# A mixture-of-experts stage that works in blocks of 64 rows instead of 128

## The chip, the cores and the metric

The kernel runs on one NeuronCore of a Trainium2 chip, in one launch. The metric is the device time of that launch in microseconds (us); lower is better. All matrices are float32.

## The reference, cut to what matters

The whole program is three layers on 512 tokens of width 1024: two sequence-mixing layers with feed-forward blocks, and a third layer that ends in a mixture of experts. Only the mixture of experts is touched:

```python
def hier_moe(h, w_rg, b_rg, w_re, b_re, w_up, w_down):    # h (512, 1024)
    g_logits = (h @ w_rg + b_rg)                          # 4 groups of 8 experts
    g_sel = jnp.argmax(g_logits, axis=-1)                 # one group per token
    e_in = ...                                            # the 8 logits of that group
    top_v, top_i = lax.top_k(e_in, 2)                     # two experts per token
    w2 = jax.nn.softmax(top_v, axis=-1) * p_sel
    combine = ...                                         # (512, 32), two non-zero shares in a row
    out = jnp.zeros_like(h)
    for n in range(32):                                   # w_up (32, 1024, 512), w_down (32, 256, 1024)
        a, b = jnp.split(h @ w_up[n], 2, axis=-1)
        out = out + combine[:, n:n + 1] * ((jax.nn.silu(a) * b) @ w_down[n])
    return out
```

A token counts for two experts only, so there are 1024 pairs of a token and an expert. The weights of one expert are 2 MiB (up) and 1 MiB (down).

How the 1024 pairs spread over the experts follows from the inputs. The reference evaluated on its own inputs gives these counts for the 32 experts: 34 39 25 25 36 34 21 36 13 24 25 30 21 16 12 33 18 16 63 38 24 15 26 24 20 87 79 45 55 41 34 15. Every expert is used; the largest counts are 87, 79 and 63.

## The kernel before, in words

The last stage, `moe` (L3286), is four steps with a barrier between them.

`route` computes the logits and the two experts of every token, and stores the normalised token rows to a DRAM buffer, `normalised_rows`.

`place` (L2909) gives each pair a slot. The slots of an expert are cut into blocks of P = 128 rows; an expert with `count` tokens gets `count/128` blocks, rounded up. From comparisons (`blocks`, L2945 to L2948, one comparison for each block that an expert may need; `full`, L2970 to L2973, the same for the rank of a token) and running sums VectorE works out `r.row` (where the result of a pair will lie), `r.expert` (the expert of each block) and the one-hot matrices `is_slot` and `is_block`. TensorE multiplies the last two (L2931) into `r.token`, the token of each slot of each block. `NB` = 40 is the number of blocks provided for; `r.before_last` says how many pairs of blocks are really filled.

`experts` (L3013) works through the filled blocks. For a block n:

- SP loads the weights of the block's expert: `load_up` (L3066, 2 MiB) and `load_down` (L3069, 1 MiB), into two sides that alternate. The load of a side is issued when the matmuls that read it two blocks earlier are done. Each block loads its weights, also where two blocks have the same expert.
- POOL gathers the block's token rows by an indirect DMA from `normalised_rows` (L3117).
- PE transposes the rows (`turn_rows`, L3131), DVE copies them out of PSUM into `e.x` (`columns`, L3217). `first` (L3141) multiplies with the up weights: the rows are the stationary operand, the 512 columns of the weights move. ACT (silu, L3185) and DVE (`gated`, L3225) make the hidden rows; PE transposes these (`turn_hidden`, L3150), ACT copies them (L3194), and `second` (L3161) multiplies with the down weights, again with 512 moving columns at a time. ACT copies the result out (L3199), and SP stores it to the DRAM buffer `expert_results` (`store`, L3076).

PE's order is a software pipeline, written out by hand:

```python
            def step(n):
                if inside(n, 1):
                    first(later(n, 1))
                turn_hidden(n)
                if inside(n, 2):
                    turn_rows(later(n, 2))
                second(n)
```

`each_block` (L3037) runs the first pair of blocks, a hardware loop over the following pairs with a branch that skips those not filled, and the last filled pair. Before that, SP runs its own loop over all pairs (L3097 to L3103): for a pair that is not filled it writes zeros to `expert_results`, for a filled one it only counts a semaphore up.

`combine` (L3239) gathers the two result rows of every token by eight indirect DMAs and adds them with their shares to the residual.

Of the kernel before, what the change touches and what calls it, by code (L numbers as in the profile page):

```python
# [18 lines left out]
F32 = mybir.dt.float32  # L19
# [7 lines left out]
P = 128  # L27
# [2876 lines left out]
SLOTS = 2 * T  # L2904
NB = 2 * -(-((SLOTS + NE * (P - 1)) // P) // 2)
FTE = EF // P


def place(k, r, zeros):  # L2909

# [3 lines left out]
    with nc.Block(no_gpsimd_drain=True) as block:  # L2914
        @block.tensor
        def _(pe):
            ps = k.ps[:, 0, :]
            for t in range(NT):

                for before in range(t):  # L2920
                    nc.tensor.matmul(ps[:, t * NE:(t + 1) * NE], k.ones[:, :], r.both[:, before, :], start=(before == 0), stop=False, skip_group_check=True)
                nc.tensor.matmul(ps[:, t * NE:(t + 1) * NE], k.tri[0][:, :], r.both[:, t, :], start=(t == 0), stop=True, skip_group_check=True)
            for t in range(NT):
                nc.tensor.matmul(ps[:, NT * NE:(NT + 1) * NE], k.ones[:, :], r.both[:, t, :], start=(t == 0), stop=(t == NT - 1), skip_group_check=True)

            nc.tensor.matmul(ps[:, (NT + 1) * NE:(NT + 1) * NE + 1], k.tri[0][:, :], k.ones[:, 0:1], start=True, stop=True,
                             skip_group_check=True).then_inc(k.pa.sem, 1)

            pe.wait_ge(*k.va(1))
            for n in range(2 * NT):  # L2930
                last = nc.tensor.matmul(k.ps[:, 1, 0:NB], r.is_slot[:, n, :], r.is_block[:, n, :], start=(n == 0), stop=(n == 2 * NT - 1))  # L2931
            last.then_inc(k.pb.sem, 1)

        @block.vector
        def _(dve):
            nc.vector.memset(zeros[:, :], 0.0)
            ps = k.ps[:, 0, :]
            upto = ps[:, 0:NT * NE].rearrange("p (t e) -> p t e", t=NT)
# [6 lines left out]
            nc.vector.tensor_scalar(r.blocks[:, :], count, 0.0, None, ALU.is_gt)  # L2945
            for n in range(1, T // P):
                dve.drain()
                nc.vector.scalar_tensor_tensor(out=r.blocks[:, :], in0=count, scalar=float(n * P), in1=r.blocks[:, :], op0=ALU.is_gt, op1=ALU.add)  # L2948
            dve.drain()
# [17 lines left out]
            dve.drain()  # L2967
            nc.vector.scalar_tensor_tensor(out=r.row_f[:, :], in0=r.block[:, :], scalar=float(P), in1=r.rank[:, :], op0=ALU.mult, op1=ALU.add)

            nc.vector.tensor_scalar(r.full[:, :], r.rank[:, :], float(P), None, ALU.is_ge)  # L2970
            for n in range(2, T // P):
                dve.drain()
                nc.vector.scalar_tensor_tensor(out=r.full[:, :], in0=r.rank[:, :], scalar=float(n * P), in1=r.full[:, :], op0=ALU.is_ge, op1=ALU.add)  # L2973
            dve.drain()
            nc.vector.tensor_tensor(r.block[:, :], r.block[:, :], r.full[:, :], ALU.add)
            nc.vector.scalar_tensor_tensor(out=r.rank[:, :], in0=r.full[:, :], scalar=-float(P), in1=r.rank[:, :], op0=ALU.mult, op1=ALU.add)
            nc.vector.tensor_copy(r.row[:, :], r.row_f[:, :])
# [21 lines left out]
            dve.wait_ge(*k.pb(1))  # L2999
            nc.vector.tensor_copy(r.token[:, :], k.ps[:, 1, 0:NB])  # L3000
    k.pa.close(1)
# [11 lines left out]
def experts(k, r, rows_dram, y_dram, up, dn, e):  # L3013
# [43 lines left out]
    with nc.Block(no_gpsimd_drain=True) as block:  # L3057
        @block.sync
        def _(sp):
# [14 lines left out]
            def store(n):  # L3074
                sp.wait_ge(e.y_ready, at_block(n, 1, 1))
                sp.dma_start(y_dram[bass.ds(at_block(n, P), P), :] if isinstance(n, tuple) else y_dram[n * P:(n + 1) * P, :],  # L3076
                             e.y[:, side(n), :]).then_inc(e.y_ended if of_last_pair(n) else e.y_stored[side(n)], 16)

# [30 lines left out]
        @block.gpsimd  # L3109
        def _(pool):  # L3110
            def step(n):
                s = side(n)
                if not early(n, 2):
                    pool.wait_ge(e.turned, at_block(n, 1, -1))
                nc.gpsimd.tensor_copy(e.slot_token[:, s:s + 1], r.token[:, bass.ds(at_block(n), 1)] if isinstance(n, tuple) else r.token[:, n:n + 1])
                pool.drain()
                nc.gpsimd.indirect_dma_start(e.rows[:, s, :], None, rows_dram, bass.IndirectOffsetOnAxis(ap=e.slot_token[:, s:s + 1], axis=0))\  # L3117
                    .then_inc(e.gathered[s], 16)

            each_block(pool, pair_before_last(nc.gpsimd), step)  # L3120
            pool.drain()

        @block.tensor
        def _(pe):
# [9 lines left out]
            def first(n):  # L3134
                s = side(n)
                pe.wait_ge(e.x_ready, at_block(n, 1, 1))
                pe.wait_ge(e.up_loaded[s], pair(n, 16))
                if not early(n, 2):
                    pe.wait_ge(e.hidden, at_block(n, 1, -1))
                for c in range(KD):  # L3140
                    last = nc.tensor.matmul(k.ps[:, UB + s, :], e.x[:, s, c, :], up[s][:, c, :], start=(c == 0), stop=(c == KD - 1))  # L3141
                last.then_inc(e.up_done, 1)
# [10 lines left out]
            def second(n):  # L3153
# [5 lines left out]
                for half in range(2):  # L3159
                    for j in range(FTE):  # L3160
                        last = nc.tensor.matmul(k.ps[:, YB + half, :], e.hid_cm[:, s, j, :], dn[s][:, j, half * BANK:(half + 1) * BANK],  # L3161
                                                start=(j == 0), stop=(j == FTE - 1))
# [16 lines left out]
        def _(act):  # L3179
            def silu(n):  # L3180
                s = side(n)
                act.wait_ge(e.up_done, at_block(n, 1, 1))
                if not early(n, 2):
                    act.wait_ge(e.hidden, at_block(n, 1, -1))
                nc.scalar.activation(e.silu[:, s, :], k.ps[:, UB + s, 0:EF], ACT.Silu).then_inc(e.silu_ready, 1)  # L3185

            def step(n):
# [4 lines left out]
                if not early(n, 2):  # L3192
                    act.wait_ge(e.down_done, at_block(n, 1, -1))
                nc.scalar.copy(e.hid_cm[:, s, :, :], k.ps[:, HB, 0:EF].rearrange("p (j m) -> p j m", j=FTE)).then_inc(e.hid_ready, 1)  # L3194
                act.wait_ge(e.down_done, at_block(n, 1, 1))
                if not early(n, 2):
                    act.wait_ge(e.y_stored[s], at_block_pairs(n))
                for half in range(2):
                    last = nc.scalar.copy(e.y[:, s, half * BANK:(half + 1) * BANK], k.ps[:, YB + half, :])  # L3199
                last.then_inc(e.y_ready, 1)  # L3200
# [8 lines left out]
        def _(dve):  # L3209
            def columns(n):  # L3210
# [75 lines left out]
def moe(k, out):  # L3286

    nc, A, sb = k.nc, k.A, k.alloc
    with ExitStack() as c:
# [14 lines left out]
        r.token_id = sb("moe_token_id", [P, NT], to=c)  # L3304
        r.is_slot = sb("moe_is_slot", [P, 2 * NT, P], to=c)
        r.is_block = sb("moe_is_block", [P, 2 * NT, NB], to=c)
# [9 lines left out]
        e.rows = sb("expert_rows", [P, 2, D], to=c)  # L3316
        e.x = sb("expert_x", [P, 2, KD, P], to=c)
        e.silu = sb("expert_silu", [P, 2, EF], to=c)
        e.hid = sb("expert_hid", [P, 2, EF], to=c)
        e.hid_cm = sb("expert_hid_cm", [P, 2, FTE, P], to=c)  # L3320
        e.zeros = sb("zeros", [P, D], to=c)
# [14 lines left out]
        place(k, r, e.zeros)  # L3336
        experts(k, r, rows_dram, y_dram, up, dn, e)
# [46 lines left out]
```

## Time and profile before

| | us |
|---|---|
| median of 3 runs | 3220.49 |
| lowest, highest run | 3217.85, 3221.48 |
| span of the profiled execution (first to last instruction) | 3219.3 |
| its own time | not given beside the span; the span is 1.2 below the median of the runs |
| PE busy | 2712.0 (84%) |
| PE weight load busy | 2062.7 (64%) |
| DVE, ACT, POOL busy | 1439.6, 991.8, 1018.6 |
| mean granted TensorE clock | 0.875 of full speed |

The table gives the sums over the span. The expert stage is about the last 420 us of it, from the first weight load of the stage at 2799.3 us. Busy shares over the whole span say little of this stage, so views of the stage by itself are needed: the profile's 40 slices (each 80.5 us), busy times by stretch, and timelines. A matmul of float32 shows as two records.

### The profile page before, as it was taken

The page shows a single profiled execution, that of the slowest core. Times are in us where ns is not written, and L with a number is a line of the kernel's source. Part 1 is how long each engine was busy: PE and PEld are TensorE (multiplying, and loading weights), DVE is VectorE, ACT ScalarE, POOL GpSimd, SP SyncE. Part 2 cuts the span into 40 slices and gives each one's busy share as a digit, 9 for nine tenths or more (in the row PEclk, how much of TensorE's full clock was granted, in tenths as well). Part 3 has the DMA queues.
Part 4 walks back from the last instruction along what each step waited for, and adds up shares of the span by engine and source line. Part 5 has one row for each costly group of instructions (what it writes and reads, how often), then busy time and mean ns, then how long its engine had stood idle before and what let it go on. Part 6 is the DMA issues. An engine that isn't in the chain of part 4 may idle for free. (4 is left out here: it accounts for less than half of the span.)

```text
span 3219.3 us, 32244 instructions
## 1 busy us (share of the span) xinstructions
PE 2712.0 (84%) x11467; PEld 2062.7 (64%) x11467; DVE 1439.6 (45%) x2067; ACT 991.8 (31%) x1675; POOL 1018.6 (32%) x673
## 2 busy tenths in 40 slices
PE   6969696869799898947779989789795978599996
PEld 5859585657688786824568878577584667444442
DVE  4468405625544443034454444417896265411111
ACT  2233331033454324331244442433332342111111
POOL 2424342034444344412234434444250053001111
PEclk9979797779899998967789999799796589599998
DMA  2300020021233312210023332222030011299997
GB/s 90 105 27 1 31 74 1 1 105 66 72 98 91 117 66 79 79 54 1 13 63 94 98 106 84 92 80 96 26 105 26 1 69 39 101 362 369 369 365 260
DMA packets 203760, 319.88 MB, mean 99 GB/s; under 512 B 13269, under 2 KB 105309, under 8 KB 203517
## 3 DMA queue, kind: packets, MB, share of 16 engines
q1 hardware_dynamic: 197885, 297.39, 27.0%
q0 software_dynamic: 5760, 20.97, 1.7%
q8 instruction: 71, 1.16, 0.1%
q14 instruction: 44, 0.36, 0.0%
HBM read 293.17 MB, written 25.17 MB: 99 GB/s over the span
## 5 line engine op out<-in xcount | busy, mean ns | idle before, releaser
L357 POOL TENSOR_TENSOR w_lo<-ring,w_hi 128x512 fp32r<-128x512 f32 (+1 forms) x264 | 355.5, 1348 | 579.2 <-ACT w_hi L514 578.6
L514 ACT CAST w_hi<-ring 128x512 fp32r<-128x512 f32 (+1 forms) x264 | 163.1, 618 | 487.6 <-PE ps L364 446.0
L357 POOL TENSOR_TENSOR ffn_w_lo<-ring,ffn_w_hi 128x1024 fp32r<-128x1024 f32 x88 | 211.5, 2426 | 275.2 <-ACT ffn_w_hi L1689 275.2
L362 PE MATMUL ps<-w_hi,h_hi 128*128 128x512 f32 (+1 forms) x672 | 264.4, 393 | 33.3 <-DVE h_lo L357 33.0
L362 PE MATMUL ps<-ffn_h_hi,ffn_w_hi 128*128 128x512 f32 x704 | 278.0, 395 | 16.3 <-DVE ffn_h_lo L357 16.3
L363 PE MATMUL ps<-ffn_h_lo,ffn_w_hi 128*128 128x512 f32 x704 | 276.8, 393 | 0.0
L364 PE MATMUL ps<-ffn_h_hi,ffn_w_lo 128*128 128x512 f32 x704 | 276.6, 393 | 0.0
L362 PE MATMUL ps<-wo_hi,lhs_hi 128*128 128x512 f32 x608 | 241.3, 397 | 41.1 <-DVE lhs_lo L357 41.1
L357 POOL TENSOR_TENSOR wo_lo<-ring,wo_hi 128x1024 fp32r<-128x1024 f32 x76 | 186.4, 2458 | 275.7 <-ACT wo_hi L642 275.7
L363 PE MATMUL ps<-w_lo,h_hi 128*128 128x512 f32 (+1 forms) x672 | 262.6, 391 | 0.0
L364 PE MATMUL ps<-w_hi,h_lo 128*128 128x512 f32 (+1 forms) x672 | 262.3, 390 | 0.0
L363 PE MATMUL ps<-wo_lo,lhs_hi 128*128 128x512 f32 x608 | 240.4, 395 | 0.0
L364 PE MATMUL ps<-wo_hi,lhs_lo 128*128 128x512 f32 x608 | 239.8, 394 | 0.0
L3141 PE MATMUL ps<-ring,expert_x 128*128 128x512 f32 x512 | 229.9, 603 | 8.9 <-issue 6.1
L3141 PEld LDWEIGHTS ps<-ring,expert_x 128*128 128x128 f32 x512 | 98.8, 194 | 134.2 <-issue 130.8
L362 PEld LDWEIGHTS ps<-w_hi,h_hi 128*128 128x128 f32 x672 | 128.4, 191 | 64.5 <-POOL w_lo L357 38.7
L362 PEld LDWEIGHTS ps<-ffn_h_hi,ffn_w_hi 128*128 128x128 f32 x704 | 133.7, 190 | 48.8 <-issue 11.1
L357 DVE TENSOR_TENSOR lhs_lo<-ffn_g,lhs_hi 128x512 fp32r<-128x512 f32 x44 | 110.1, 2509 | 119.5 <-ACT lhs_hi L643 119.5
L1731 DVE SCALAR_TENSOR_TENSOR y_tmp<-ps,pcol,y_tmp 128x511 f32<-128x511 f32 x88 | 61.9, 746 | 220.1 <-ACT y_tmp L1694 220.1
L362 PEld LDWEIGHTS ps<-wo_hi,lhs_hi 128*128 128x128 f32 x608 | 116.6, 192 | 67.5 <-POOL wo_lo L357 42.8
L642 ACT CAST wo_hi<-ring 128x1024 fp32r<-128x1024 f32 x76 | 79.7, 1049 | 258.1 <-PE ps L364 253.5
L362 PE MATMUL ps<-h_hi,w_hi 128*128 128x512 f32 x352 | 142.3, 404 | 16.7 <-DVE h_lo L357 16.0
(529 smaller groups left out, 5282.0 us busy)
## 6 DMA issues: line engine op xcount, KB each, us to landing
ring<-in_w_up SPq DMA_DIRECT2D x32, 2048.0 KB, 12.1
ring<-in_ffn_w_up SPq DMA_DIRECT2D x88, 512.0 KB, 4.9
moe_down<-in_w_down SPq DMA_DIRECT2D x32, 1024.0 KB, 10.1
ring<-in_ab_w_in SPq DMA_DIRECT2D x13, 2048.0 KB, 7.8
ring<-in_w_in SPq DMA_DIRECT2D x11, 2048.0 KB, 7.8
ring<-in_ffn_w_down SPq DMA_DIRECT2D x10, 2048.0 KB, 8.0
expert_results<-expert_y SPq DMA_DIRECT2D x32, 512.0 KB, 10.2
ring<-in_c_w_in SPq DMA_DIRECT2D x6, 2048.0 KB, 8.3
```

The lines of the kernel that those rows point to most:

```text
L357: return engine.tensor_tensor(lo, whole, hi.bitcast(F32), ALU.subtract)
L362: nc.tensor.matmul(out, left[0], right[0], start=start, stop=False, **more)
L363: nc.tensor.matmul(out, left[0], right[1], start=False, stop=False, **more)
L364: return nc.tensor.matmul(out, left[1], right[0], start=False, stop=stop, **more)
L514: nc.scalar.copy(part(w_hi, p), chunk(j)[:, rows, cols]).then_inc(k.w_hi_ready.sem, 1)
L642: nc.scalar.copy(w_hi[:, n % PIECES, :], weights(n)).then_inc(k.w_hi_ready.sem, 1)
L1731: nc.vector.scalar_tensor_tensor(out=ybuf[:, s, half, 1:T], in0=bank(s, half)[:, 0:T - 1], scalar=column(tap0, i, s, half), in1=ybuf[:, s, ...
L3141: last = nc.tensor.matmul(k.ps[:, UB + s, :], e.x[:, s, c, :], up[s][:, c, :], start=(c == 0), stop=(c == KD - 1))
```

## The change: blocks of 64 rows

A constant `ROWS` = 64 takes the place of P = 128 wherever a block's height is meant. `NB`, the number of blocks provided for, becomes 48. Each expert with more than 64 tokens now takes two blocks, and each of these loads the expert's weights. The weights, the moving columns of the matmuls and the order of the work on each engine stay. The gather, the store, the silu, the product and the copies of the result work on 64 partitions; the copies of `e.x` and `e.hid_cm` take half of the columns. The two kinds of transposes still turn full 128-row tiles, whose lower half is set to zero once, by two memsets in `place`. `place` has four more comparisons for `blocks` and four more for `full`. `combine` is as before.

```diff
 SLOTS = 2 * T
-NB = 2 * -(-((SLOTS + NE * (P - 1)) // P) // 2)
+ROWS = 64
+NB = 2 * -(-((SLOTS + NE * (ROWS - 1)) // ROWS) // 2)
...
-                last = nc.tensor.matmul(k.ps[:, 1, 0:NB], r.is_slot[:, n, :], r.is_block[:, n, :], ...)
+                last = nc.tensor.matmul(k.ps[0:ROWS, 1, 0:NB], r.is_slot[:, n, :], r.is_block[:, n, :], ...)
...
             nc.vector.memset(zeros[:, :], 0.0)
+            nc.vector.memset(rows[ROWS:P, :, :], 0.0)
+            nc.vector.memset(hid[ROWS:P, :, :], 0.0)
...
-            for n in range(1, T // P):
+            for n in range(1, T // ROWS):
                 dve.drain()
-                nc.vector.scalar_tensor_tensor(out=r.blocks[:, :], in0=count, scalar=float(n * P), ...)
+                nc.vector.scalar_tensor_tensor(out=r.blocks[:, :], in0=count, scalar=float(n * ROWS), ...)
...
-            for n in range(2, T // P):
+            for n in range(2, T // ROWS):
                 dve.drain()
-                nc.vector.scalar_tensor_tensor(out=r.full[:, :], in0=r.rank[:, :], scalar=float(n * P), ...)
+                nc.vector.scalar_tensor_tensor(out=r.full[:, :], in0=r.rank[:, :], scalar=float(n * ROWS), ...)
...
-                nc.vector.tensor_scalar(r.is_slot[:, n, :], r.iota[:, :], r.rank[:, n:n + 1], None, ALU.is_equal)
+                nc.vector.tensor_scalar(r.is_slot[:, n, :], r.iota[:, 0:ROWS], r.rank[:, n:n + 1], None, ALU.is_equal)
...
-                             e.y[:, side(n), :]).then_inc(...)
+                             e.y[0:ROWS, side(n), :]).then_inc(...)
...
-                    sp.dma_start(y_dram[bass.ds(i * (2 * P) + 2 * P, 2 * P), :].rearrange("(s p) d -> p s d", p=P),
-                                 e.zeros[:, :].rearrange("p (o d) -> p o d", o=1).to_broadcast([P, 2, D])).then_inc(e.y_zeroed, 16)
+                    sp.dma_start(y_dram[bass.ds(i * (2 * ROWS) + 2 * ROWS, 2 * ROWS), :].rearrange("(s p) d -> p s d", p=ROWS),
+                                 e.zeros[0:ROWS, :].rearrange("p (o d) -> p o d", o=1).to_broadcast([ROWS, 2, D])).then_inc(e.y_zeroed, 16)
...
-                nc.gpsimd.indirect_dma_start(e.rows[:, s, :], None, rows_dram, ...e.slot_token[:, s:s + 1]...)
+                nc.gpsimd.indirect_dma_start(e.rows[0:ROWS, s, :], None, rows_dram, ...e.slot_token[0:ROWS, s:s + 1]...)
...
-                    last = nc.tensor.matmul(k.ps[:, UB + s, :], e.x[:, s, c, :], up[s][:, c, :], ...)
+                    last = nc.tensor.matmul(k.ps[0:ROWS, UB + s, :], e.x[:, s, c, :], up[s][:, c, :], ...)
...
-                        last = nc.tensor.matmul(k.ps[:, YB + half, :], e.hid_cm[:, s, j, :], dn[s][:, j, half * BANK:(half + 1) * BANK], ...)
+                        last = nc.tensor.matmul(k.ps[0:ROWS, YB + half, :], e.hid_cm[:, s, j, :], dn[s][:, j, half * BANK:(half + 1) * BANK], ...)
...
-                nc.scalar.activation(e.silu[:, s, :], k.ps[:, UB + s, 0:EF], ACT.Silu).then_inc(e.silu_ready, 1)
+                nc.scalar.activation(e.silu[0:ROWS, s, :], k.ps[0:ROWS, UB + s, 0:EF], ACT.Silu).then_inc(e.silu_ready, 1)
...
-                nc.scalar.copy(e.hid_cm[:, s, :, :], k.ps[:, HB, 0:EF].rearrange("p (j m) -> p j m", j=FTE)).then_inc(e.hid_ready, 1)
+                nc.scalar.copy(e.hid_cm[:, s, :, :], k.ps[:, HB, 0:EF].rearrange("p (j m) -> p j m", j=FTE)[:, :, 0:ROWS]).then_inc(e.hid_ready, 1)
...
-                    last = nc.vector.tensor_copy(e.x[:, s, c, :], k.ps[:, XB + half, :].rearrange("p (c m) -> p c m", c=NT))
+                    last = nc.vector.tensor_copy(e.x[:, s, c, :], k.ps[:, XB + half, :].rearrange("p (c m) -> p c m", c=NT)[:, :, 0:ROWS])
...
-                nc.vector.tensor_tensor(e.hid[:, s, :], e.silu[:, s, :], k.ps[:, UB + s, EF:2 * EF], ALU.mult).then_inc(e.hidden, 1)
+                nc.vector.tensor_tensor(e.hid[0:ROWS, s, :], e.silu[0:ROWS, s, :], k.ps[0:ROWS, UB + s, EF:2 * EF], ALU.mult).then_inc(e.hidden, 1)
...
-        y_dram = nc.dram_tensor("expert_results", (NB * P, D), F32, kind="Internal").ap()
+        y_dram = nc.dram_tensor("expert_results", (NB * ROWS, D), F32, kind="Internal").ap()
```

## Rows read from the trace of the kernel before

**Rows 1.** The page: granted TensorE clock and DMA rate in 40 slices.

```profile
PEclk9979797779899998967789999799796589599998
GB/s 90 105 27 1 31 74 1 1 105 66 72 98 91 117 66 79 79 54 1 13 63 94 98 106 84 92 80 96 26 105 26 1 69 39 101 362 369 369 365 260
```

**Rows 2.** Stretches: PE, PEld, DVE, ACT, POOL busy us (count), clock, DMA share, GB/s.

```profile
3000.00:3050.00 50.00, 50.00 (x148) 24.45 (x147) 7.99 (x14) 7.99 (x18) 5.67 (x10) 1.00 1.01 373
...
2825.00:2830.00 5.00, 5.00 (x14) 2.19 (x13) 0.00 (x0) 0.00 (x0) 0.00 (x0) 1.00 1.03 415
```

**Rows 3.** Timeline of one block on PE: start us, us, engine, line, operation.

```profile
3003.01 7.03 PE L3141 MATMUL ps<-ring,expert_x 128*128 128x512 f32 x16
...
3009.87 0.38 PE L3150 MATMUL ps<-ident,expert_hid 128*128 128x128 f32 x2
...
3010.09 1.04 PE L3131 MATMUL ps<-ident,expert_rows 128*128 128x128 f32 x8
...
3010.97 3.60 PE L3161 MATMUL ps<-moe_down,expert_hid_cm 128*128 128x512 f32 x8
3014.40 7.03 PE L3141 MATMUL ps<-ring,expert_x 128*128 128x512 f32 x16
```

**Rows 4.** Timeline: an early and the last issue of an up load, 26 blocks apart.

```profile
2862.09 0.37 SPq L3066 DMA_DIRECT2D ring<-in_w_up  x1
...
3158.34 0.37 SPq L3066 DMA_DIRECT2D ring<-in_w_up  x1
```

**Rows 5.** DMA issues of the stage: count, KB each, median us to landing.

```profile
ring<-in_w_up SPq DMA_DIRECT2D x32, 2048.0 KB, 12.1
...
expert_results<-expert_y SPq DMA_DIRECT2D x32, 512.0 KB, 10.2
...
expert_rows<-normalised_rows,expert_slot_token POOLq DMA_INDIRECT x32, 8.0
```

**Rows 6.** Matmuls on 128 and on 16 stationary columns: duration ns min/median/max.

```profile
L3141 PE MATMUL ps<-ring,expert_x x512: 592/592/1219, 2811.6 to 3180.4; 128*128 128x512 f32 x171
...
L478 PE MATMUL ps<-h_cm,ring x32: 592/593/603, 1379.4 to 1392.7; 128*16 128x512 f32 x32
```

**Rows 7.** Timeline of the start of the experts, up to the third block's matmuls.

```profile
2811.57 9.05 PE L3141 MATMUL ps<-ring,expert_x 128*128 128x512 f32 x16 [1.38 <-DVE expert_x L3217]
...
2818.85 4.06 SPq L3099 DMA_DIRECT2D expert_results<-zeros  x4
...
2824.70 6.51 SPq L3066 DMA_DIRECT2D ring<-in_w_up  x2
...
2830.94 3.60 PE L3161 MATMUL ps<-moe_down,expert_hid_cm 128*128 128x512 f32 x8
...
2840.68 9.84 PE L3141 MATMUL ps<-ring,expert_x 128*128 128x512 f32 x16 [6.15 <-issue]
```

**Rows 8.** The zero fill's issues on SP: durations in ns, first and last start.

```profile
L3099 SPq DMA_DIRECT2D expert_results<-zeros x4: 383/404/432, 2818.9 to 2822.5; - x4
```

**Rows 9.** Timeline of the step that places the slots.

```profile
2777.88 0.91 DVE L2936 MEMSET zeros<- 128x1024 f32 x1 [0.97 <-PEq L2805]
...
2783.85 0.19 DVE L2945 TENSOR_SCALAR moe_blocks<-ps 128x32 f32<-128x32 f32 x1 [4.48 <-PE ps L2926]
2784.13 0.72 DVE L2948 SCALAR_TENSOR_TENSOR moe_blocks<-ps,moe_blocks 128x32 f32<-128x32 f32 x3
...
2788.00 0.41 DVE L2973 SCALAR_TENSOR_TENSOR moe_full<-moe_rank,moe_full 128x8 f32<-128x8 f32 x2
...
2792.57 1.49 DVE L2986 TENSOR_TENSOR moe_ended<-moe_block_end,moe_iota 128x1280 f32<-128x1280 f32 x1
2794.11 3.49 PEld L2931 LDWEIGHTS ps<-moe_is_block,moe_is_slot 128*128 128x128 f32 x16 [10.38 <-DVE moe_ended L2986]
...
2797.79 0.20 DVE L3000 CAST moe_token<-ps 128x40 int32<-128x40 f32 x1 [1.27 <-PE ps L2931]
```

**Rows 10.** Landing times of the result stores: min/median/max us.

```profile
DMA to landing us min/median/max: 2.7/10.2/15.3
```

More of the change, by code:

```diff
@@ L2904, with place @@
 SLOTS = 2 * T
-NB = 2 * -(-((SLOTS + NE * (P - 1)) // P) // 2)
+ROWS = 64
+NB = 2 * -(-((SLOTS + NE * (ROWS - 1)) // ROWS) // 2)
 FTE = EF // P
-def place(k, r, zeros):
+def place(k, r, zeros, rows, hid):
     nc = k.nc
@@ L2930, in _ @@
             for n in range(2 * NT):
-                last = nc.tensor.matmul(k.ps[:, 1, 0:NB], r.is_slot[:, n, :], r.is_block[:, n, :], start=(n == 0), stop=(n == 2 * NT - 1))
+                last = nc.tensor.matmul(k.ps[0:ROWS, 1, 0:NB], r.is_slot[:, n, :], r.is_block[:, n, :], start=(n == 0), stop=(n == 2 * NT - 1))
             last.then_inc(k.pb.sem, 1)
@@ L2945, in _ @@
             nc.vector.tensor_scalar(r.blocks[:, :], count, 0.0, None, ALU.is_gt)
-            for n in range(1, T // P):
+            for n in range(1, T // ROWS):
                 dve.drain()
-                nc.vector.scalar_tensor_tensor(out=r.blocks[:, :], in0=count, scalar=float(n * P), in1=r.blocks[:, :], op0=ALU.is_gt, op1=ALU.add)
+                nc.vector.scalar_tensor_tensor(out=r.blocks[:, :], in0=count, scalar=float(n * ROWS), in1=r.blocks[:, :], op0=ALU.is_gt, op1=ALU.add)
             dve.drain()
@@ L2999, in _ @@
             dve.wait_ge(*k.pb(1))
-            nc.vector.tensor_copy(r.token[:, :], k.ps[:, 1, 0:NB])
+            nc.vector.tensor_copy(r.token[0:ROWS, :], k.ps[0:ROWS, 1, 0:NB])
     k.pa.close(1)
@@ L3114, in step @@
                     pool.wait_ge(e.turned, at_block(n, 1, -1))
-                nc.gpsimd.tensor_copy(e.slot_token[:, s:s + 1], r.token[:, bass.ds(at_block(n), 1)] if isinstance(n, tuple) else r.token[:, n:n + 1])
+                nc.gpsimd.tensor_copy(e.slot_token[0:ROWS, s:s + 1], r.token[0:ROWS, bass.ds(at_block(n), 1)] if isinstance(n, tuple) else r.token[0:ROWS, n:n + 1])
                 pool.drain()
-                nc.gpsimd.indirect_dma_start(e.rows[:, s, :], None, rows_dram, bass.IndirectOffsetOnAxis(ap=e.slot_token[:, s:s + 1], axis=0))\
+                nc.gpsimd.indirect_dma_start(e.rows[0:ROWS, s, :], None, rows_dram, bass.IndirectOffsetOnAxis(ap=e.slot_token[0:ROWS, s:s + 1], axis=0))\
                     .then_inc(e.gathered[s], 16)
@@ L3140, in first @@
                 for c in range(KD):
-                    last = nc.tensor.matmul(k.ps[:, UB + s, :], e.x[:, s, c, :], up[s][:, c, :], start=(c == 0), stop=(c == KD - 1))
+                    last = nc.tensor.matmul(k.ps[0:ROWS, UB + s, :], e.x[:, s, c, :], up[s][:, c, :], start=(c == 0), stop=(c == KD - 1))
                 last.then_inc(e.up_done, 1)
@@ L3160, in second @@
                     for j in range(FTE):
-                        last = nc.tensor.matmul(k.ps[:, YB + half, :], e.hid_cm[:, s, j, :], dn[s][:, j, half * BANK:(half + 1) * BANK],
+                        last = nc.tensor.matmul(k.ps[0:ROWS, YB + half, :], e.hid_cm[:, s, j, :], dn[s][:, j, half * BANK:(half + 1) * BANK],
                                                 start=(j == 0), stop=(j == FTE - 1))
@@ L3198, in step @@
                 for half in range(2):
-                    last = nc.scalar.copy(e.y[:, s, half * BANK:(half + 1) * BANK], k.ps[:, YB + half, :])
+                    last = nc.scalar.copy(e.y[0:ROWS, s, half * BANK:(half + 1) * BANK], k.ps[0:ROWS, YB + half, :])
                 last.then_inc(e.y_ready, 1)
@@ L3304, in moe @@
         r.token_id = sb("moe_token_id", [P, NT], to=c)
-        r.is_slot = sb("moe_is_slot", [P, 2 * NT, P], to=c)
+        r.is_slot = sb("moe_is_slot", [P, 2 * NT, ROWS], to=c)
         r.is_block = sb("moe_is_block", [P, 2 * NT, NB], to=c)
@@ L3333, in moe @@
         rows_dram = nc.dram_tensor("normalised_rows", (T, D), F32, kind="Internal").ap()
-        y_dram = nc.dram_tensor("expert_results", (NB * P, D), F32, kind="Internal").ap()
+        y_dram = nc.dram_tensor("expert_results", (NB * ROWS, D), F32, kind="Internal").ap()
         route(k, wr, r, k.ytmp[:, :, :], rows_dram)
-        place(k, r, e.zeros)
+        place(k, r, e.zeros, e.rows, e.hid)
         experts(k, r, rows_dram, y_dram, up, dn, e)
```

16 lines of the change are left out of this document (8 added, 8 removed).

## The prediction, made before the changed kernel ran

> **What bounds the kernel now.** I read the 40 slices first. In the last five the DMA rate jumps from about 100 to 360 to 370 GB/s [rows 1]: this is the expert stage, and at first sight it is bound by transfers. The second view corrects that. In the 50 us from 3000 the DMA engines are busy all the time (share 1.01), but PE is busy for 50.00 of 50.00 us too, at the full granted clock (1.00, the 2.4 GHz level) [rows 2]. Two resources at 100% need a third view that tells which one sets the pace. In the timeline of one block the matmuls of `first` start at 3003.01, the transposes of the hidden rows at 3009.87, those of the token rows at 3010.09, `second` at 3010.97, and the next `first` at 3014.40 [rows 3]. Nowhere does a row of PE carry a wait for a DMA. The steps add up by themselves: 16 records of `first` in 6.86 us are 0.429 us each; 8 of `second` in 3.43 us are 0.429 each; the ten transposes take 1.10 us. That is 11.39 us, the whole period. Over 26 blocks the period does not vary: (3158.34 - 2862.09) / 26 = 11.394 us [rows 4].
>
> The transfers have slack that the share of 1.01 hides. A block moves 2 MiB + 1 MiB of weights, 0.5 MiB of gathered rows and 0.5 MiB of results, 4.19 MB, in 11.39 us: 368 GB/s. Shortly after the start of the stage the same engines moved 415 GB/s [rows 2]. An up load is issued when `first` of its side is done and is needed 11.39 + 4.3 = 15.7 us later; it lands after 12.1 us [rows 5]. So PE bounds the steady part, and the transfers follow some 10% behind as second. Only at the start do transfers bind: PE has finished `second` of block 0 at about 2834.5, waits 6.15 us, and starts block 2's `first` at 2840.68 [rows 7].
>
> **The change part by part.**
>
> *Number of blocks.* The counts of tokens of the experts are 87 and 79 for two, 63 or less for the others. At 128 rows that is 32 blocks, as the 512 records of L3141 (16 for a block) show [rows 6]. At 64 rows it is 34 blocks, 17 pairs, so nothing is lost to pairing.
>
> *Time of a block on PE.* The rows are the stationary operand and the weights move, so the 64 rows halve the loaded columns, not the 512 that move. The trace has the same matmul with 16 stationary columns: 593 ns, against 592 ns with 128 [rows 6]. 32 of them start within 1379.4 to 1392.7, 13.3 us / 31 = 0.429 us apart, the cadence of the expert matmuls. The weight load of 0.19 us lies beneath them (PE weight load 24.45 of 50 us [rows 2]) and shortening it gives nothing. The transposes still turn 128 rows, so their 1.10 us stay. A block costs 11.39 us as before. Bounds: the row with 16 columns leaves no room above or below; I give it 0.05 us either way.
>
> *What gets shorter and lies aside.* The copies of `e.x` and of `e.hid_cm`, silu and the product run on ACT and DVE, which are each busy for 7.99 of 50 us [rows 2]: worth nothing. The gather and the store move half of the bytes. A block moves 3.67 MB in place of 4.19, 322 GB/s at the period of 11.39 us. PE does not wait for these transfers now, so their relief in the steady part is worth nothing as well. All in all the stage moves 34 x 3.67 MB = 124.8 in place of 134.2 MB, 7% less, and this shows only in the DMA columns.
>
> *Sum of the steady part:* 2 x 11.394 = +22.8 us.
>
> *Start of the stage.* Here bytes count, until block 2's up weights land. What SP does there: its loop counts filled pairs (now 16 at the head of the loop instead of 15) and then issues a zero fill for each pair that is not filled. Provided are 24 pairs, 17 filled, so 7 fills of 0.5 MiB instead of 4 of 1 MiB: 3.67 against 4.19 MB. The fills start 1.2 us apart (2818.9 to 2822.5 for four [rows 8]), so the last of seven starts three steps, 3.6 us, later, and the up load queued behind them is issued at about 2829 instead of 2824.70 [rows 7].
> Lower end: 64-row transfers run at the full rate of about 0.4 MB/us. Up to block 2's first matmul 0.52 MB of fills and four gathers of 0.26 MB fall away, 1.57 MB or 3.9 us. By 2829 the queue has just run dry, the load takes 2.1 / 0.4 = 5.2 us and some 2 us to land: 2836.3, 4.4 us earlier than now. After so short a wait the granted clock might stay at full; now block 2's `first`, behind its wait of 6.15 us, takes 9.84 us against 7.03 for a steady one [rows 3, 7], another 2.8 us. Together -7.2 us.
> Upper end: each 64-row transfer takes as long as its counterpart of 128 rows. Then the seven fills take 7/4 of the four: four are 4.19 MB / 0.4 = 10.5 us, seven are 18.3 us. From 2819.5 they end at about 2838, gathers in between 2838.5, the load lands about 2845: +4.3 us.
> The two ends are 11.5 us apart, and the trace has no transfer of such size on 64 partitions. The nearest row is the wait as it is, 6.15 us: fewer bytes on one side, more and later issues on the other. I take 0 and keep -7.2 and +4.3.
>
> *Placing the slots.* These are in series with the whole stage. Four more comparisons for `blocks`: three of them take 2784.13 to 2784.93 with their drains, 0.27 each, so +1.07. Four more for `full` at 0.245 each (L2973 has two in 0.49 us): +0.98. `ended` grows from 1280 to 1536 elements: 1.49 x 48/40 = +0.30 [rows 9]. Against that the eight comparisons into `is_slot` are half as wide (0 to -0.5, I take -0.3), and the product at L2931 loads 64 columns: its 3.49 us of weight loads may fall to half, but then DVE's reduction and four small operations beside it (together 1.8 + 0.9 us after the signal) end last. Of the 3.7 us from signal to copy [rows 9] up to 0.9 can go; I take -0.6. The two memsets (2048 and 512 elements in the lower partitions, by the 0.91 us for 1024 about 1.8 + 0.5 us) fall into the 4.48 us for which DVE waits for PE [rows 9]: nothing, and their cover is twice what they need. Sum +1.4 us, between +0.6 and +2.4.
>
> *End of the stage.* Before `combine` can gather, the last store has to land; unhindered that takes 2.7 us for 0.5 MiB [rows 10]. With half the bytes 0 to -0.7 us: I take -0.2. `combine` reads the same 4 MiB as before.
>
> *Sum:* 22.8 + 0 + 1.4 - 0.2 = +24.0 us. Against the profiled span of 3219.3 this gives 3243.3; the span is 1.2 below the runs' median of 3220.49, which is within their spread of 3.6, so I add it: **3244.5 us**, 0.75% slower.
>
> **The rivals.**
>
> *A. The start gains.* The 64-row transfers run at the full rate, and the wait before block 2 all but disappears: 22.8 - 7.2 + 1.4 - 0.4 = +16.6, 3237 us. For it: the bytes. Against it: the seven issues of SP.
>
> *B. A 64-row transfer takes as long as one of 128 rows.* Then the seven fills hold the queue for 18.3 us: 22.8 + 4.3 + 1.4 = +28.5, 3249 us. In the steady part nothing changes: gather and store then take what they take now, and PE does not wait for that. The trace speaks neither for nor against. The Trainium skill does: its page "SBUF — State Buffer", section "Door 1: The DMA port swizzle", says that partitions 0 to 63 reach only 8 of the 16 ports, so that such a transfer runs at about half of the rate. By that rule the result is this rival's; no run here shows it yet.
>
> *C. The other sign: transfers set the period, not PE.* If the matmuls with 64 stationary columns ran faster, or if PE's records only looked full while it waited for weights, the period would follow the bytes: 3.67/4.19 x 11.39 = 9.98 us, and 34 x 9.98 = 339 against 32 x 11.39 = 364.5 us: -25 + 1.4, about 3197 us. It decides from the point where the cadence falls below 0.370 us for a record. For it: the DMA share of 1.01. Against it: no wait for a DMA in a steady block, a period constant to 0.01 us, and the row with 16 columns at the same duration.
>
> *D. It does not do what it says.* The expert with 63 tokens is one short of the edge. If rounding moved two tokens to it, there would be 35 blocks, 18 pairs, 36 blocks run: +22.8 more, 3267 us. The margins between second and third choice in that group are wide (one token under 0.09), so this is unlikely.
>
> **How the numbers follow.** Forecast 0.42 (own range 3240 to 3247), A 0.20, B 0.26, C 0.05, D 0.03, others 0.04, in which half is slower. The range goes from below A to above B with the bounds of the placing step: 3233 to 3253. Within 0.2% (6.4 us, about what a measurement tells from no change) is nearly none of them: 0.02. Faster 0.06, the rest slower, 0.92.
>
> **What would show it.** In the changed kernel: 544 records of L3141, 34 up loads and 7 zero fills; a period of 11.39 us between issues of L3066, with PE at 50.00 of 50 us and a rate near 322 GB/s; records of `first` and `second` still 0.429 us apart; the third block's `first` at about its present distance from the stage's first load, 41.4 us (A: 37, B: 46); 1.4 us more from the first comparison of `blocks` to the copy of `r.token`. A DMA share clearly below 1 in the steady part speaks against B, one that stays at 1 for it. A wait for a DMA in a steady block, or a period other than 11.39, would make the prediction wrong.

## The result and the profile after

| | before | after |
|---|---|---|
| median of 4 runs, us | 3220.98 | 3262.38 |
| lowest, highest | 3217.85, 3222.75 | 3260.06, 3262.77 |
| ratio to before, 95% interval | | 1.0128 [1.0114, 1.0142] |
| span of the profiled execution | 3219.3 | 3258.3 |
| records of the up matmuls, zero fills | 512, 4 | 544, 7 |

The changed kernel is 41.4 us slower, 39.0 us by the two profiled spans. 18 us of that were not in the forecast of 3244.5, and the time lies above the stated range.

The first view is the middle of the stage in busy times by stretch, with the columns of [rows 2]; behind it, from the timeline, an early and the last issue of an up load, 28 blocks apart.

```profile
3000.00:3050.00 50.00, 50.00 (x145) 18.14 (x144) 4.67 (x12) 7.85 (x18) 4.42 (x8) 1.00 0.97 320
...
2868.18 0.39 SPq L3069 DMA_DIRECT2D ring<-in_w_up  x1
...
3195.41 0.38 SPq L3069 DMA_DIRECT2D ring<-in_w_up  x1
```

PE is busy for 50.00 of 50 us at full clock, and the rate has fallen from 373 to 320 GB/s: all as forecast. But the period is (3195.41 - 2868.18) / 28 = 11.687 us, not 11.394 [rows 4]. The count of records says it too: 145 fit into 50 us in place of 148. The timeline of one block on PE (the counterpart of [rows 3]) shows where the 0.29 us lie:

```profile
3001.20 7.03 PE L3144 MATMUL ps<-ring,expert_x 128*64 128x512 f32 x16
...
3008.16 0.44 PE L3153 MATMUL ps<-ident,expert_hid 128*128 128x128 f32 x2
...
3008.43 1.04 PE L3134 MATMUL ps<-ident,expert_rows 128*128 128x128 f32 x8
...
3009.40 3.65 PE L3164 MATMUL ps<-moe_down,expert_hid_cm 128*64 128x512 f32 x8
...
3012.89 7.03 PE L3144 MATMUL ps<-ring,expert_x 128*64 128x512 f32 x16
```

From start to start the four steps take 6.96, 0.27, 0.97 and 3.49 us; before they took 6.86, 0.22, 0.88 and 3.43. Within `first` nothing changed, its records are still 0.429 us apart. The difference sits where the shape of the weights changes between 128*64 and 128*128, and the row of weight loads (PEld) tells what happens there. First the kernel before, then the one after, around the start of the transposes of the hidden rows:

```profile
3009.45 0.14 PEld L3150 LDWEIGHTS ps<-ident,expert_hid 128*128 128x128 f32 x1 [0.24 <-issue]
3009.88 0.14 PEld L3150 LDWEIGHTS ps<-ident,expert_hid 128*128 128x128 f32 x1 [0.29 <-issue]
```

```profile
3007.21 0.14 PEld L3144 LDWEIGHTS ps<-ring,expert_x 128*64 128x64 f32 x1 [0.29 <-issue]
3008.16 0.20 PEld L3153 LDWEIGHTS ps<-ident,expert_hid 128*128 128x128 f32 x2 [0.81 <-issue]
```

Before, the first transpose starts at 3009.87 and its weights were loaded from 3009.45, beneath the last matmul of `first`. After, the last load of `first` is at 3007.21, and the next begins at 3008.16, together with the transpose that it belongs to. No load was drawn ahead across the change of width, and the array waits for it. The way back, from the transposes to `second`, costs as much: of the 0.29 us, 0.15 lie in the first two steps (0.10 and 0.05) and 0.15 in the last two (0.09 and 0.06). PE's own busy row hides this, because a matmul's record goes on to its modelled end: 50.00 of 50 us in both kernels.

The trace of the kernel before has such a seam too, in front of the run of 16 columns in [rows 6]:

```profile
1378.85 0.19 PEld L364 LDWEIGHTS ps<-w_hi,h_lo 128*128 128x128 f32 x1
1379.07 0.39 PE L364 MATMUL ps<-w_hi,h_lo 128*128 128x512 f32 x1
1379.39 0.11 PEld L478 LDWEIGHTS ps<-h_cm,ring 128*16 128x16 f32 x2 [0.35 <-issue]
```

The records of 128 columns start 0.227 us apart there, each load one record ahead. The first load of 16 columns starts together with its own matmul at 1379.39, 0.09 us behind the point (1379.30) that the cadence gives. It is a single case in which other things change as well, so it proves nothing by itself, but it was the place to look.

The start of the stage, from the timeline (the counterpart of [rows 7]), and the stretch in which the fills run:

```profile
2819.16 13.63 SPq L3102 DMA_DIRECT2D expert_results<-zeros  x7
...
2834.88 3.04 SPq L3069 DMA_DIRECT2D ring<-in_w_up  x2
...
2846.67 9.63 PE L3144 MATMUL ps<-ring,expert_x 128*64 128x512 f32 x16 [13.36 <-issue]
...
2825.00:2830.00 5.00, 5.00 (x20) 2.13 (x19) 0.64 (x2) 0.64 (x2) 0.10 (x1) 1.00 0.98 246
```

The same five microseconds that moved 415 GB/s before [rows 2] move 246 GB/s, with the engines as busy (0.98). The seven issues take 13.63 us in all, more than seven steps of 1.2 us would be [rows 8]; I read this as SP waiting for room in its queue, and zeros_32_96 bears on it below. Block 2 starts 47.7 us behind the first load of the stage (2798.96), where it was 41.4.

The placing step, from its timeline (the counterpart of [rows 9]), and the last row of this section, a pause that the kernel before does not have:

```profile
2782.86 1.79 DVE L2951 SCALAR_TENSOR_TENSOR moe_blocks<-ps,moe_blocks 128x32 f32<-128x32 f32 x7
...
2787.79 1.37 DVE L2976 SCALAR_TENSOR_TENSOR moe_full<-moe_rank,moe_full 128x8 f32<-128x8 f32 x6
...
2794.90 1.94 PE L2932 MATMUL ps<-moe_is_block,moe_is_slot 128*64 128x48 f32 x16 [12.35 <-DVE moe_ended L2989]
...
2797.49 0.19 DVE L3003 CAST moe_token<-ps 64x48 int32<-64x48 f32 x1
```

```profile
3213.38 7.08 PE L3144 MATMUL ps<-ring,expert_x 128*64 128x512 f32 x16 [1.66 <-issue]
```

From the first comparison to the copy of `r.token` it is 14.9 us against 13.9 [rows 9]. The pause of 1.66 us stands in front of the last block's `first`, where PE's loop has just passed over the pairs that are not filled.

The 39.0 us between the spans by landmark: up to the stage's first load -0.3 (this execution ran 1.3 us ahead before placing began, which itself took 1.0 longer); from there to block 2's `first` +6.3; from there to the last `second` +33.3, of which two blocks of 11.69 are 23.4, the longer periods of the others 8.2 (28 x 0.293), and the pause is 1.7; behind that -0.3. The runs' medians differ by 2.4 us more; the profiled execution was the shortest of its kernel (3260.06), the others took 3262.4 to 3262.8.

### The profile page after: what moved, and what is told of

It reads as the page before. It is cut to its first block and busy times, and to the rows that moved or that the text cites. A ratio compares the mean times of both kernels' runs of the same rounds, so it can differ in the third digit from the quotient of the medians.

```text
span 3258.3 us, 32594 instructions
## 1 busy us (share of the span) xinstructions
PE 2742.2 (84%) x11535; PEld 2025.9 (62%) x11535; DVE 1429.2 (44%) x2083; ACT 992.8 (30%) x1683; POOL 1013.6 (31%) x677
## 5 line engine op out<-in xcount | busy, mean ns | idle before, releaser
L3144 PE MATMUL ps<-ring,expert_x 128*64 128x512 f32 x544 | 243.5, 601 | 16.7 <-issue 15.0
L3144 PEld LDWEIGHTS ps<-ring,expert_x 128*64 128x64 f32 x544 | 75.2, 139 | 179.0 <-issue 176.7
L3228 DVE TENSOR_TENSOR expert_hid<-expert_silu,ps 64x256 f32<-64x256 f32 x34 | 14.0, 412 | 356.9 <-ACT expert_silu L3188 356.9
```

The costliest lines, as they stand in the source:

```text
L3144: last = nc.tensor.matmul(k.ps[0:ROWS, UB + s, :], e.x[:, s, c, :], up[s][:, c, :], start=(c == 0), stop=(c == KD - 1))
L3228: nc.vector.tensor_tensor(e.hid[0:ROWS, s, :], e.silu[0:ROWS, s, :], k.ps[0:ROWS, UB + s, EF:2 * EF], ALU.mult).then_inc(e.hidden, 1)
```

## Experiments

Two theories for the period: W, PE draws no weight load ahead over a change between 64 and 128 stationary columns; D, the 64-partition transfers or the shorter copies shift the block's timing. For the start: P, transfers on partitions 0 to 63 are slow; I, seven issues of SP set it. Times are medians, with the ratio to the kernel before on the same chip; that kernel took 3221.46 in the first four experiments and 3220.26 in the others. Where a time is set against the changed kernel (3262.38, beside 3220.98 for the kernel before), the two come from different series, and such a difference of 4 us alone is not clear of the spread; there the distances within the traces decide.

### full_width: both matmuls load 128 columns again

```diff
-        e.x = sb("expert_x", [P, 2, KD, ROWS], to=c)
+        e.x = sb("expert_x", [P, 2, KD, P], to=c)
-                    last = nc.tensor.matmul(k.ps[0:ROWS, UB + s, :], e.x[:, s, c, :], up[s][:, c, :], ...)
+                    last = nc.tensor.matmul(k.ps[:, UB + s, :], e.x[:, s, c, :], up[s][:, c, :], ...)
... (the same for e.hid_cm and second; both copies take all columns)
```

> The changed kernel, but the copies into e.x and e.hid_cm take all 128 columns again and the matmuls of first and second load 128 stationary columns (the upper 64 are the zero rows); gather, silu, product and store stay at 64 rows. Theory W (the period grew from 11.39 to 11.69 us because PE changes between 64 and 128 stationary columns twice in a block, and a weight load is not drawn ahead over such a change): the period is 11.39 us again, the first load of the transposes starts 0.4 us before they do, and the run is 34 x 0.29 = 10 us faster than the changed kernel, about 3252 us. Rival D (the transfers on 64 partitions, or the shorter copies, shift the block's timing): the period stays at 11.69 us and the time at 3262. The start of the stage is not touched: block 2's first matmul 47.7 us behind the first load in both.

Measured: 3254.06 us, ratio 1.0094 [1.0074, 1.0113], 8.3 us faster than the changed kernel. The issues of the up loads are back at (3190.79 - 2871.75) / 28 = 11.394 us, and in the timeline of the weight loads the one for the first transpose is drawn ahead again: it starts at 3007.70, the transpose at 3008.13:

```profile
3007.70 0.14 PEld L3153 LDWEIGHTS ps<-ident,expert_hid 128*128 128x128 f32 x1 [0.24 <-issue]
3008.13 0.14 PEld L3153 LDWEIGHTS ps<-ident,expert_hid 128*128 128x128 f32 x1 [0.29 <-issue]
```

The transfers were as in the changed kernel, so they are not the cause; the copies were whole again, and that half of D is left to the next experiment. Block 2 starts 48.0 us behind the first load, so the start is as it was. The 10 us expected were too many: the seams of blocks 0 and 1 lie ahead of block 2's wait, which hides them, and in the last two blocks PE waits for ACT anyway. From block 2's `first` to the last `second` of the changed kernel they cost 8.8 us (30 x 0.293), and the pause before the last block grew from 1.66 to 1.95 us, by just what the period lost. That leaves 8.5 us, and 8.3 were measured.

### narrow_before: only the width, in the kernel before

```diff
-                    last = nc.tensor.matmul(k.ps[:, UB + s, :], e.x[:, s, c, :], up[s][:, c, :], ...)
+                    last = nc.tensor.matmul(k.ps[0:64, UB + s, :], e.x[:, s, c, 0:64], up[s][:, c, :], ...)
... (the same for second)
```

> The kernel before (blocks of 128 rows, 32 blocks, all transfers on 128 partitions), but first and second load only 64 stationary columns and write 64 rows; the upper half of each block is left out of these matmuls. Theory W: the period becomes 11.69 us with nothing else changed, 32 x 0.29 = +9.5 us on the time before, about 3230. Rival D: 11.39 us and 3221.

Measured: 3230.92 us, ratio 1.0029 [1.0015, 1.0044], +9.5 us. The period is (3165.74 - 2861.88) / 26 = 11.687 us. So the width alone, with 128-row transfers, whole copies, 32 blocks and everything else as before, gives the changed kernel's period to the last digit, and D falls. That the time meets the 9.5 us so exactly is in part luck: from block 2's `first` to the last `second` the trace is 8.3 us longer, and the interval reaches from 5 to 14 us. The kernel leaves out the upper half of each block, so it serves as a measurement only.

### second_full: one of the two matmuls wide

```diff
-                        last = nc.tensor.matmul(k.ps[0:ROWS, YB + half, :], e.hid_cm[:, s, j, :], ...)
+                        last = nc.tensor.matmul(k.ps[:, YB + half, :], e.hid_cm[:, s, j, :], ...)
... (e.hid_cm with P columns, copied whole)
```

> The changed kernel with 128 stationary columns in second alone (e.hid_cm copied whole); first keeps 64. If each change of width costs (theory W), there are still two in a block, from first to the transposes and from second to first: the period stays at 11.65 to 11.7 us, the gap at the transposes stays, the one between the transposes and second goes and a new one stands between second and first. If it is the narrow matmuls that cost, 8 of 24 records are wide again and the period falls to about 11.6 us or, if the cost is in second alone, to 11.5. Time 3262 by W, 3256 to 3259 by the other.

Measured: 3265.72 us, ratio 1.0137 [1.0119, 1.0154], not told apart from the changed kernel's 1.0128 [1.0114, 1.0142]; period (3193.02 - 2865.73) / 28 = 11.689 us. A third of the narrow records is gone and nothing is won: the cost is by change of width, two in a block, about 0.147 us each, and not by narrow matmul. The weight loads show the gap moved from the front of `second` to its end:

```profile
3009.46 0.19 PEld L3164 LDWEIGHTS ps<-moe_down,expert_hid_cm 128*128 128x128 f32 x1 [0.24 <-issue]
3010.41 0.19 PEld L3144 LDWEIGHTS ps<-ring,expert_x 128*64 128x64 f32 x2 [0.76 <-issue]
```

### zeros_128: the fills read 128 partitions

```diff
-                    sp.dma_start(y_dram[...].rearrange("(s p) d -> p s d", p=ROWS),
-                                 e.zeros[0:ROWS, :].rearrange("p (o d) -> p o d", o=1).to_broadcast([ROWS, 2, D])).then_inc(e.y_zeroed, 16)
+                    sp.dma_start(y_dram[...], e.zeros[:, :]).then_inc(e.y_zeroed, 16)
```

> The changed kernel, but each zero fill of two blocks (128 result rows, 0.5 MiB) reads 128 partitions in place of twice 64; count, bytes and place of the fills stay. Theory P (a transfer on partitions 0 to 63 runs at about half of the rate: the trace shows 206 to 263 GB/s while the fills run, against 391 to 415 before the change): the rate returns to about 400 GB/s, the seven issues take some 8 us instead of 13.6, the up load behind them is issued at 29 to 30 us behind the first load of the stage instead of 35.9, and block 2 starts 37 to 39 us behind it instead of 47.7; with the clock kept at full 9 to 12 us faster than the changed kernel, about 3252. Rival I (seven issues of SP set it): block 2 starts at 46 to 48 us as now, and the time stays at 3262. The period stays at 11.69 us.

Measured: 3257.78 us, ratio 1.0112 [1.0095, 1.0130]. Two rows of the timeline and one stretch:

```profile
2819.20 7.29 SPq L3102 DMA_DIRECT2D expert_results<-zeros  x7
...
2828.50 2.11 SPq L3069 DMA_DIRECT2D ring<-in_w_up  x2
...
2825.00:2830.00 5.00, 5.00 (x13) 1.43 (x12) 0.00 (x0) 0.00 (x0) 0.00 (x0) 1.00 1.02 389
```

The seven issues take 7.29 us, the rate is 389 GB/s, and the up load goes out 30.1 us behind the first load (2798.39), all as P says; I falls as the whole cause. The edit changes two things, though: the partitions, and one run for each fill in place of two. The next experiment parts them. The next step of the expectation was wrong: block 2 starts at 2842.15, 43.8 us behind the first load, not 37 to 39. The up load needs 13.7 us from issue to use, where I had counted some 8, as for a transfer by itself. In a steady block of the changed kernel an up load lands after 11.0 us (median), with the other transfers beside it. Nor did the clock stay up: block 2's `first` takes 9.82 us. The start wins 3.9 us. That is clear of its own noise (47.7, 48.0 and 48.2 us in the traces of the changed kernel, full_width and second_full), and about what the medians show (4.6). 2.4 us of the start's loss stay (43.8 against 41.4 in the kernel before): the up load still goes out 30.1 us behind the first load, where it was 25.4.

### zeros_32_96: the same fills from other partitions

```diff
-                                 e.zeros[0:ROWS, :].rearrange("p (o d) -> p o d", o=1)...
+                                 e.zeros[32:32 + ROWS, :].rearrange("p (o d) -> p o d", o=1)...
```

> The changed kernel, with one edit: the 64 partitions that each zero fill reads are 32 to 95 in place of 0 to 63. Shape, bytes, count and place of the fills are unchanged. Theory P1 (it matters which partitions: 0 to 63 reach half of the ports, 32 to 95 all of them): the seven issues take 7.3 us as with 128 partitions instead of 13.6, the rate while they run is 370 to 390 GB/s, and block 2 starts about 43.8 us behind the first load instead of 47.7; 4 us faster than the changed kernel. Rival P2 (it matters that there are only 64 partitions, or two runs for each): issues 13.6 us, 206 to 263 GB/s, 47.7 us, the same time as the changed kernel.

Measured: 3258.83 us, ratio 1.0120 [1.0104, 1.0137], 3.5 us below the changed kernel. The last three lines are the fills' issues by themselves, in ns (minimum, median, maximum), of the changed kernel, zeros_128 and this one.

```profile
2821.11 9.40 SPq L3102 DMA_DIRECT2D expert_results<-zeros  x7
...
2844.26 9.82 PE L3144 MATMUL ps<-ring,expert_x 128*64 128x512 f32 x16 [9.34 <-issue]
...
2825.00:2830.00 5.00, 5.00 (x12) 1.37 (x10) 0.00 (x0) 0.00 (x0) 0.93 (x1) 1.00 1.01 364
...
L3102 SPq DMA_DIRECT2D expert_results<-zeros x7: 619/1339/1794, 2819.2 to 2831.0; - x7
...
L3102 SPq DMA_DIRECT2D expert_results<-zeros x7: 332/332/402, 2819.2 to 2826.2; - x7
...
L3102 SPq DMA_DIRECT2D expert_results<-zeros x7: 607/607/776, 2821.1 to 2829.9; - x7
```

Same shape, same bytes, same number of partitions, and 364 GB/s in place of 246. Block 2 starts 43.8 us behind the first load (2800.47), like zeros_128. The issues took 9.4 us, more than the 7.3 I had written and less than 13.6. Their single durations say why: a fill in two runs of 64 partitions takes SP 0.61 us to issue where one of 128 partitions takes 0.33, and that is the 2.1 us to zeros_128. In the changed kernel the shortest issue takes 0.62 us as well, the median one 1.34: the 4.2 us more come with the slow transfers, which fits SP waiting for room. So it matters which 64 partitions a transfer touches, and P2 falls but for the dearer issue. The section "Door 1: The DMA port swizzle" of "SBUF — State Buffer" in the Trainium skill has this: partitions 0 to 63 reach 8 of the ports, and by its table of ports 32 to 95 reach all 16. The traces agree in kind; the pure rate of such a fill was not isolated, since gathers ran beside it.

### nb36: room for 36 blocks

```diff
-NB = 2 * -(-((SLOTS + NE * (ROWS - 1)) // ROWS) // 2)
+NB = 36
```

> The changed kernel with room for 36 blocks instead of 48, enough for the 34 of these inputs: one pair is skipped and filled with zeros in place of seven. Theory S (the start's loss is the fills ahead of block 2's load; the pause of 1.66 us on PE before the last block's matmuls is the seven skipped turns of its loop): the up load is issued about 24.5 us behind the first load instead of 35.9, block 2 starts at 34 to 36 us instead of 47.7 with the clock at full (2.6 us more), the pause before the last block is gone (-1.7), placing is 0.5 us shorter: 16 to 19 us faster than the changed kernel, 3243 to 3246. Rival: the start is bound by the weights and gathers themselves and stays above 43 us, or the pause has another cause and stays; then 3255 or more. The period stays at 11.69 us.

Measured: 3242.65 us, ratio 1.0067 [1.0049, 1.0085], 20 us faster than the changed kernel by the medians and 17 by the profiled spans, at the edge of the 16 to 19 expected. The up load goes out 22.4 us behind the first load, earlier than expected. In the timeline block 2 starts 34.7 us behind the first load (2799.65) with no wait before it and at full clock, and the last block follows without a pause:

```profile
2834.31 7.03 PE L3144 MATMUL ps<-ring,expert_x 128*64 128x512 f32 x16
...
3196.59 7.03 PE L3144 MATMUL ps<-ring,expert_x 128*64 128x512 f32 x16
```

(3196.59 - 2834.31) / 31 = 11.686 us: from block 2 to block 33 nothing is left but the period. The size of the provision, `NB`, had cost about 16 us at the start (13.0 of waiting and 2.6 of clock) and 1.7 us at the end. 36 fits only these inputs, so this is an experiment and not a version to use.

### late_zeros_before: the fills behind the last weight load

The kernel before, with its loop of fills moved behind the last weight load, between the two last blocks' steps on SP. The counting loop stays where it was.

```diff
         step((before, 2, 4))
+        between()
         step((before, 3, 4))
...
-                with sp.If(before < i):
-                    sp.dma_start(y_dram[...]..., e.zeros...).then_inc(e.y_zeroed, 16)
...
+            def fill():
+                with sp.Fori(0, NB // 2 - 1) as i:
+                    with sp.If(before < i):
+                        sp.dma_start(y_dram[...]..., e.zeros...).then_inc(e.y_zeroed, 16)
-            each_block(sp, before, step)
+            each_block(sp, before, step, fill)
```

> The kernel before (128 rows) with the four zero fills issued after the last weight load of the stage, when the transfer engines run empty, instead of ahead of block 2's load. Theory S: block 2's wait of 6.15 us goes and its first matmuls run at full clock (-2.8 us), the last stores come 0 to 2 us later: 7 to 9 us faster than the kernel before, about 3212. Rival: block 2's load is late for another reason (the weights of blocks 0 and 1 and the gathers), and the wait stays above 4 us; then no more than 2 us are won, or the fills delay the last stores by what is won at the start.

Measured: 3215.79 us, ratio 0.9984 [0.9975, 0.9993], the fastest of all, by 2 to 8 us below the kernel before. Block 2's wait is gone: three `first` follow at 2823.56, 2835.05 and 2846.45 at full clock. But the fills are not free at the end:

```profile
2835.05 7.03 PE L3146 MATMUL ps<-ring,expert_x 128*128 128x512 f32 x16
...
3175.20 4.01 SPq L3105 DMA_DIRECT2D expert_results<-zeros  x4
...
3192.47 0.94 POOL L3253 DMA_INDIRECT ring<-expert_results,moe_row  x1 [50.89 <-PEq L3248]
```

`combine`'s first gather comes 13.9 us behind the start of the last `second` (3178.55); in the kernel before it was 9.5 us (3196.51 - 3186.98). The end waits for the last stores and for 4 MiB of zeros: in the 5 us from 3180 the transfer engines are full (share 1.02, 405 GB/s), where in the kernel before they moved 105 GB/s in the 5 us from 3185. 4.4 of the 9 us won at the start are given back. The expectation of 0 to 2 us was too low, and the net of 4.5 us falls short of the 7 to 9 expected.

### late_full: both repairs in the 64-row kernel

The edits of full_width, zeros_128 and the late fills together.

> The 64-row kernel with both repairs: 128 stationary columns in first and second, and the zero fills on 128 partitions behind the last weight load. What is left over the kernel before with late fills is the two blocks (22.8 us), the placing (1.0) and the pause of 1.9 us before the last block. Expected 3236 to 3240, some 25 us above the kernel before with late fills. If the transfers that are saved were worth anything once the start is free of fills, it would be closer than 20 us.

Measured: 3238.74 us, ratio 1.0053 [1.0038, 1.0068]. That is 23.0 us above late_zeros_before, where the two blocks alone are 22.8. The pause before the last block is still there:

```profile
3193.00 7.13 PE L3148 MATMUL ps<-ring,expert_x 128*128 128x512 f32 x16 [1.95 <-issue]
...
3206.12 3.70 PE L3168 MATMUL ps<-moe_down,expert_hid_cm 128*128 128x512 f32 x8 [1.28 <-ACT expert_hid_cm L3201]
...
3216.03 0.96 POOL L3255 DMA_INDIRECT ring<-expert_results,moe_row  x1 [49.10 <-PEq L3250]
```

That the total comes to just the two blocks is a balance of other terms. By the traces, from block 2's `first` to the last `second` it is 25.0 us longer than late_zeros_before (two blocks, and the pause); up to block 2's `first` it is 2.6 longer; and from the last `second` to `combine`'s first gather it takes 9.9 us instead of 13.9, 4.0 less. There, behind the last weight load, fewer bytes (3.67 MB of zeros in place of 4.19, stores of half the size) may be worth something; the fills are also issued 1.5 us earlier against the last `second`, and no run separates the two. In the steady part the bytes that are saved bring nothing: the period is 11.394 us with either.

## Why the prediction was wrong, point by point

*PE bounds the stage.* Right. With 12% fewer bytes in a block the stage did not get faster, and rival C fell.

*Number of blocks, +22.8.* Right: 34 blocks, 17 pairs, two more periods. Rival D, more blocks than 34, did not occur.

*Time of a block on PE, "11.39 us as before ... 0.05 us either way".* This step failed, and it is the largest miss: the period grew by 0.293 us, 8.8 us over the 30 blocks in which no wait hides it. The row with 16 stationary columns was read rightly: the cadence inside a run of equal matmuls does not depend on the width. But [rows 6] are a run of one shape. I took from it that "shortening the weight load gives nothing" and did not ask what lies at the seams, where a block now goes from 64 to 128 columns and back. narrow_before and full_width show that the seams are all of it, second_full that it is the change of width that costs. The start of that very run, at 1379.39, had the sign of it.

*Start of the stage, taken as 0 between -7.2 and +4.3.* This term failed as well. It measured +6.3, above the upper end. The larger part of it, 3.9 us, is rival B's mechanism, shown by zeros_128 and zeros_32_96: fills from partitions 0 to 63 run slowly and hold the queue. The other 2.4 us stay with fast fills; there the up load goes out 4.7 us later than in the kernel before, behind seven issues in place of four, and the saved bytes do not make up for it. I had both mechanisms and the bound of 18.3 us for the fills, and took the middle without a row for it. The 2.0 us beyond that bound are not separated further: SP's seven issues took 13.6 us, so the up load went out at 2834.88 and not at 2829, and block 2 started 11.8 us behind it, where I had given a load 7 us by itself.

*Placing, +1.4.* It measured +1.0, within its bounds; the product that makes `r.token` took 1.94 us in place of 3.64, and DVE ended last, as described. *End, -0.2.* -0.3. The two memsets were hidden: DVE still waited for 1.55 us afterwards.

*Not in the sum at all: the pause of 1.66 us.* PE's loop skips seven unfilled pairs instead of four. I had counted the skipped turns for SP alone. There is no pause with four skipped pairs (the kernel before) or one (nb36), and with seven it stays when the fills are moved away (late_full, 1.95 us). What PE's queue does in such a turn no run shows.

By the profiled spans, +39.0 against +24.0, the miss of 15.0 us is: seams 8.8, start 6.3, pause 1.7, placing -0.4, end -0.1, and -1.3 by which this execution was ahead before the stage. Rival B came closest with 3249; B with the seams (8.8) and the pause (1.7) is 3259.5, and with the 2.0 us more at the start 3261.5.

## What to carry to other kernels

Cutting a block's height pays only if the height is what is paid for. Where the rows are the stationary operand and the weights move, a half-filled block costs the same on TensorE (0.429 us a record at 128, 64 and 16 columns here), and each extra block costs a full period; count the blocks first. When one operand's shape shrinks, look at the seams between instructions of different shape: padding the narrow operand back to the common width can be the faster form. Ask also of a transfer that keeps its bytes but loses partitions, and of every bound that a provision such as `NB` puts on loops that run in front of the real work.

## What the runs showed of the hardware that was not expected

A change between 64 and 128 stationary columns costs about 0.147 us at full clock, in either direction, beside matmuls of 512 moving columns: periods of 11.686 to 11.689 us in six kernels with two changes in a block, 11.394 us in the kernel before, full_width, late_zeros_before and late_full with none. The load behind the change starts together with its own matmul (both at 3008.16 in the changed kernel, and both at 3009.40 on the way back), not one record ahead.

In seven fills of 0.5 MiB the transfers ran with 206 to 263 GB/s from partitions 0 to 63 (the four stretches of 5 us from 2820 to 2840), 336 and 364 GB/s from 32 to 95 and 369 and 389 GB/s from all 128 (the two from 2820 to 2830), with gathers beside them.
